# Feed-forward gate and up: narrow products of one column block placed between the wide products of the next

## The reference, cut to what matters

```python
def swiglu_ffn(h, w_gate, w_up, w_down):
    return (jax.nn.silu(h @ w_gate) * (h @ w_up)) @ w_down
```

## Time and profile before

| | |
|---|---|
| median of three runs | 2421.52 us |
| span of the profiled execution, first to last instruction | 2419.4 us |
| median less span | 2.1 us |
| granted TensorE clock, mean | 0.999 |
| TensorE products, busy | 2398.0 us |
| VectorE busy | 1893.5 us |
| ScalarE busy | 1440.4 us |

### The profile page before, as it was taken

The page is one execution under the profiler, slowest core; times in us unless marked ns, Lnnn a source line. Parts: engine busy times, 40 slices in busy tenths (PEclk is TensorE's granted clock), DMA queues, the critical chain, the costliest instruction groups (busy, mean ns, idle before and its releaser), DMA issues.

```text
span 2419.4 us, 34411 instructions
## 1 busy us (share of the span) xinstructions
PE 2398.0 (99%) x12612; PEld 2031.4 (84%) x12612; DVE 1893.5 (78%) x1989; ACT 1440.4 (60%) x1477; POOL 6.5 (0%) x30
## 2 busy tenths in 40 slices
PE   8999999999999999999999999999999999999998
PEld 7788899888888888888888888888888888887887
DVE  7667686678988898889888988676966676688766
ACT  6645444567777777777777777455254454543444
POOL 1000000000000000000000000000000000000000
PEclk9999999999999999999999999999999999999999
DMA  8375142469999999999999996853355566533653
GB/s 299 117 248 184 61 139 71 148 211 378 363 373 336 362 364 376 337 362 359 380 336 370 361 373 227 284 197 122 131 175 190 185 232 226 174 129 123 194 192 126
DMA packets 314239, 593.76 MB, mean 245 GB/s; under 512 B 8880, under 2 KB 134960, under 8 KB 313904
## 3 DMA queue, kind: packets, MB, share of 16 engines
q1 hardware_dynamic: 314160, 592.70, 69.5%
HBM read 591.62 MB, written 1.05 MB: 245 GB/s over the span
## 4 chain that ended last, share of the span: by engine, by line
PE 94%; DVE 3%; ACT 1%; DMA 1%; DVEq 1%; issue 0%; SPq 0%; ACTq 0%
PE bank L203 20%; PE bank L204 19%; PE bank L205 19%; PE bank L1216 16%; PE bank L1220 8%; PE bank L3454 1%; PE bank L2943 1%; PE bank L3381 1%; PE bank L2228 1%; PE bank L2238 1%; DMA mslot<-in_e_w_in 1%; PE bank L2918 1%; PE bank L1712 1%; PE bank L1056 0%; PE bank L2147 0%; PE bank L2247 0%
## 5 line engine op out<-in xcount | busy, mean ns | idle before, releaser
L3184 DVE TENSOR_TENSOR weights_lo<-mslot,weights_hi 128x2048 fp32r<-128x2048 f32 x336 | 768.2, 2291 | 110.8 <-ACT weights_hi L3086 110.5
L3086 ACT ACTIVATE weights_hi<-mslot 128x2048 fp32r<-128x2048 f32 x336 | 644.2, 1920 | 228.4 <-PE bank L205 228.4
L1368 DVE TENSOR_TENSOR weights_lo<-scratch,weights_hi 128x2048 fp32r<-128x2048 f32 x165 | 377.3, 2289 | 166.5 <-ACT weights_hi L1361 166.4
L1216 PE MATMUL bank<-x_parts,weights_hi 128*128 128x512 f32 x1760 | 441.2, 393 | 1.8 <-DVE x_parts L919 1.8
L1216 PEld LDWEIGHTS bank<-x_parts,weights_hi 128*128 128x128 f32 x1760 | 319.5, 189 | 63.7 <-DVE x_parts L919 2.4
L203 PE MATMUL bank<-weights_hi,x_pair 128*128 128x512 f32 x896 | 356.6, 398 | 0.2 <-issue 0.2
L204 PE MATMUL bank<-weights_lo,x_pair 128*128 128x512 f32 x896 | 351.7, 393 | 0.0
L205 PE MATMUL bank<-weights_hi,x_pair 128*128 128x512 f32 x896 | 349.4, 390 | 0.0
L1361 ACT ACTIVATE weights_hi<-scratch 128x2048 fp32r<-128x2048 f32 x165 | 315.2, 1913 | 50.2 <-PE bank L205 49.2
L203 PE MATMUL bank<-weights_hi,hidden_hi 128*128 128x512 f32 x808 | 315.9, 391 | 0.0
L204 PE MATMUL bank<-weights_lo,hidden_hi 128*128 128x512 f32 x808 | 315.2, 390 | 0.0
(11 more groups left out here) (550 smaller groups left out, 2789.5 us busy)
## 6 DMA issues: line engine op xcount, KB each, us to landing
mslot<-in_o_moe_w_gate SPq DMA_DIRECT2D x112, 1024.0 KB, 5.5
mslot<-in_o_moe_w_up SPq DMA_DIRECT2D x112, 1024.0 KB, 5.6
mslot<-in_o_moe_w_down SPq DMA_DIRECT2D x112, 1024.0 KB, 5.7
scratch<-in_ffn_w_gate SPq DMA_DIRECT2D x44, 1024.0 KB, 5.4
scratch<-in_ffn_w_up SPq DMA_DIRECT2D x44, 1024.0 KB, 5.4
scratch<-in_ffn_w_down SPq DMA_DIRECT2D x44, 1024.0 KB, 5.1
mslot<-in_o_w_in SPq DMA_DIRECT2D x7, 2048.0 KB, 8.7
scratch<-in_e_ffn_w_gate SPq DMA_DIRECT2D x11, 1024.0 KB, 5.4
```

Of the source, the lines that this page charges most:

```text
L1216: pe.matmul(m.ps[bank + j][:, :], hi[:, k, cols(j)], both, start=(k == 0), stop=False)
L1368: dve.tensor_tensor(m.wlo[to][:, :], m.fslot[i], m.whi[to][:, :], ALU.subtract).then_inc(m.sig["f_lo"], 1)
L3086: act.activation(m.whi[(place + half) % PLACES][:, :], r.slot[slot + half], ACT.Copy).then_inc(s["r_hi"], 1)
L3184: dve.tensor_tensor(m.wlo[i][:, :], r.slot[slot + half], m.whi[i][:, :], ALU.subtract).then_inc(s["r_lo"], 1)
```

## The change

It reorders the 32 products of a call of `inner` that is not `arriving`. Block 0's wide products come first, as before. Then each narrow product of block 0 is followed by a wide product of block 1, eight times, and then come block 1's narrow products. Number, shapes, operands and waits stay.

```diff
-        for j in tiles:
-            for k in range(KT):
-                wide(j, k)
-            if j == 0:
-                split_in(kind, u)
-                if row_scale:
-                    rows_spread()
-            narrow(j, range(KT)).then_inc(s[done], 1)
+        for k in range(KT):
+            wide(0, k)
+        split_in(kind, u)
+        if row_scale:
+            rows_spread()
+        for k in range(KT):
+            last = narrow(0, [k])
+            if k == KT - 1:
+                last.then_inc(s[done], 1)
+            wide(1, k)
+        narrow(1, range(KT)).then_inc(s[done], 1)
```

## The result

The change made the kernel slower by a little: 2425.07 us median (2424.07 to 2426.8, 21 runs) against 2421.58 us for the kernel before (2421.11 to 2423.63, 21 runs), a ratio of 1.0015 with a 95% interval of 1.0008 to 1.0021. That is 3.5 us. The forecast was 2 us less than before.

What follows compares the result with a forecast made beforehand. TensorE's rate of taking products was taken to bound the kernel. The single term, 840 x (0.347 - 0.3494) = -2.0 us, on the median 2421.5 gave 2419.5 us, range 2412.5 to 2425.5 us.

Steps and rivals of the forecast that it cites:

- What bounds the kernel: Whole kernel: TensorE, busy 2398.0 of 2419.4 us, sets the time by the distance between starts of its products.
- The pair, the one term: Eight turns in each of 105 calls: 840 narrow-wide pairs at 0.347 instead of 0.3494 us, -2.0 us.
- settled paces for both: Pair in the turns: wide product at 0.227 and narrow at 0.120 us, 0.347 together, with no effect of the switch.
- an exchange: Pair in the turns: cheap narrow and dear wide steps offset, 0.3437 to 0.350 us; forecast 2419.5 us, chance 0.58.
- closing narrow run: Last narrow run of a call: keeps a wide product as its neighbour, costed at no change.
- The forecast's own range: Time of the changed kernel if the forecast case holds: 2416.7 to 2422.0 us.
- the wide product pays each time: Rival for the turns: full excess at each switch, narrow at 0.120, pair 0.355 to 0.360, 2426.2 to 2430.4 us; chance 0.10.
- The change of bank: Turns: each step goes to the other PSUM bank; no cost for wide products, unknown for narrow ones.
- Loads: Before each product: one load ahead, pace at least 0.106 us; nearly level with narrow products, time to spare in wide runs.
- Release of block 0: Up call: last narrow product starts 1.6 us later, ScalarE's copy comes about 1.1 us before block 1's; costs nothing.
- clock: TensorE's clock stays at 1.00 in all three stages; the rival of half clock in the turns, 2714 us, chance 0.01.
- down stages: Stages after gate and up: stay at 5.47 us.

Runs made afterwards that it cites:

- the half loads: 64 of 128 weight columns: in narrow products of the kernel before (2413.3 us), or in the changed kernel's wide products in the turns (2415.8 us).
- both kinds halved: Changed kernel with 64 of 128 weight columns in both wide (k = 1 to 7) and narrow (k = 1 to 6) products of the turns; 2417.7 us.
- other slices: Changed kernel with block 0's narrow products taken in the order of slices 4 to 7, 0 to 3; 2425.01 us, ratio 1.0012.
- twos: Changed kernel with two narrow products of block 0, then two wide ones of block 1, four times; 2421.0 us, ratio 0.9997.
- fours: Changed kernel with narrow products of block 0 and wide ones of block 1 alternating in groups of four; 2422.89 us, ratio 1.0003.
- runs of sixteen: Kernel before, with sixteen wide then sixteen narrow products per call: 2422.0 us in all calls, 2419.92 us with groups 0 and 1 left as before.

## Why the prediction was wrong

**What bounds the kernel**: right. The whole difference is in distances between starts of products; no wait appeared.

**The pair, the one term**: this step failed. It put a pair in turns at 0.347 us, between 0.340 and 0.36, and 0.353 was measured in 101 of 105 calls. The bounds held, the choice between them did not. The sum went by settled paces for both, 0.227 + 0.120, "the one that needs no effect of the switch". In the cycle the wide steps average 236 ns, 9 more, and the narrow ones 117, 3 less. The other reading, an exchange at 0.235 + 0.113 = 0.348, had the wide steps nearly right (236) and the narrow ones 4 ns too low: the cheap 113 comes at every third turn, not at each. Both readings took a step for a property of two neighbours. The rows already showed five dear steps in a row, so the state outlasts a step, and the four calls at 0.347 show that the state at the start of the turns decides what they cost. For these four the number was right, for no reason that the prediction gave. The term -2.0 us should have been 105 x 33 ns = +3.5 us, and 3 of the 33 ns lie in the closing narrow run, which was costed at no change.

That 2425.07 us lies inside the stated range, 0.4 us under its upper end, is owed to the width of the range. The forecast's own range ended at 2422.0.

**The rival that came nearest** was the one in which the wide product pays each time. It decided from 0.3551 and lay at 2426.2 to 2430.4; the measured pair falls between its edge and the forecast's 0.350, a stretch that no case had. The wide half of its mechanism, a lasting disturbed state, is what the trace shows; its narrow half, a step that stays at 0.120, is not.

**The change of bank**: right, costs nothing (turns inside one bank have the same cycle; equal lengths in two banks run at 227). The idea that the 120 of a narrow run comes from one bank is wrong: with half loads the run averages 114 in one bank.

**Loads**: "loads and products are nearly level in a narrow run" is confirmed by the half loads, and the rows had it more closely than 0.106. The first of the sixteen steps of 8 columns is 25 ns and the other fifteen are 111 to 112, so full loads follow each other every 112 ns there, and half of a settled wide step is 113. "In a wide run the load has time to spare" is true of a settled run and misled for the turns: there a shorter load under a wide product gains too. The Trainium skill ("TensorE: Matmul & The Clock Gate", section "Step-by-step: what each phase is for") has the next load run beneath the running product on a read port of its own, so that it takes no read bandwidth from it. The trace shows no port. A settled wide step is 227 ns with a full load beneath it, and 227 for a half-size wide product with a half load (both kinds halved), which agrees. But a narrow step of a run falls from 120 to 113 with a half load beneath it, and in turns the mean wide step falls from 236 to 229, so a load beneath is not free there.

**Release of block 0, clock, down stages**: right. The copy comes 1.13 us ahead of the other (1.1 expected), the clock is 1.00, down takes 5.47.

**What is shown, and what is open.** Shown: for turns that are entered from a settled wide run, the excess needs steps of unequal length and full loads together. Equal lengths remove it (512 columns), half-size wide products, with half loads under the narrow ones, remove it; staying in one bank, other slices and a longer narrow product (320 columns) do not, and weight buffers in turns cost nothing where the lengths are equal. (The turns in one bank were entered from a narrow run.) Shown by comparing calls, with no run of its own: entered otherwise, the same turns cost 0.347. Open: how load and stream disturb each other inside TensorE, and why the cycle has three turns. Unequal lengths are also not the only thing that keeps a stream from settling. In the kernel before, a stretch of products of another stage (L203 to L205), all 512 wide and without a wait, never reaches 227:

```profile
484.33 0.39 PE L204 MATMUL bank<-mix_parts,weights_lo 128*128 128x512 f32 x1
...
489.42 0.39 PE L205 MATMUL bank<-weights_lo 128*128 128x512 f32 x1
```

That is 5.09 us for 22 steps, 0.231 each, in a cycle of three again (231, 234, 228 ns); why is open. The steps cannot be summed from a cost per switch, since twos are cheaper than fours.

## What to carry to other kernels

Where TensorE is dense, judge an order by start-to-start distances, and look at every call, not at one: the same turns took 0.353 in 101 calls and 0.347 in four. Single turns were the dearest order tried and turns of two as cheap as runs of sixteen (0.348), so do not expect a cost per switch. Do not price a new pattern from its pairs of neighbours if the rows show an effect that lasts longer than one step; give the range the whole gap between cases. When a wait is moved to gain such nanoseconds, list every product that stands behind it: here one row-scale product, sent 1.4 us later in one network, took back 1.4 us.

## What the runs showed of the hardware that was not expected

- In turns of single narrow (256 columns) and wide (512) products with loads of 128 columns, entered from a settled wide run, the steps form a cycle of three pairs: 113, 232, 118, 241, 120, 236 ns (101 of 105 calls of the changed kernel). Turns in one bank, entered from a narrow run, show the same cycle.
- Entered from a wide run that has not settled, or right behind the row-scale products, the same turns run at 117 and 230 ns (the other four calls).
- In a run of narrow products a step is 113 ns with a load of 64 columns beneath it and 120 with one of 128.
- Products of 8 columns with a load of 128 columns each follow each other every 111 to 112 ns (kernel before, from the second step of the earlier trace rows on).
- A wide run after a narrow one takes 233, 236, 228, 233, 231 ns before it settles at 227, whether the narrow run had full or half loads in its middle. After turns of single products it takes 236 and is settled.
- With the narrow product at 320 columns the turns take 147 and 229 to 233 ns; with 512 columns all take 227.
- A run of products that are all 512 columns wide can stay in a cycle of 231, 234, 228 ns for over twenty steps (kernel before, from 484.33 us on).
